# Half-size weight splits in the slots of the first attention, and the first softmax tile's scores ahead of the last lead-in block

## The reference, cut to what matters

```python
z = h @ w_in
c_q, c_kv, k_pe, fq, fk, fv, f_logit = split(z)
q  = (rms_norm(c_q, g_cq) @ w_uq)           # 8 MLA heads, 96 wide
kv = (rms_norm(c_kv, g_ckv) @ w_ukv)        # k_nope, v_mla
o_mla = blocked_causal_attention(q, k, v_mla, scale)
o_fox = blocked_causal_attention(qf, kf, vf, scale, cum_log_f)   # 8 "fox" heads, 64 wide
out = concatenate([o_mla, o_fox]) @ w_out
```

## Time and profile before

| | us |
|---|---|
| median of 3 runs | 1318.15 |
| lowest and highest of them | 1315.78, 1324.64 |
| the profiled execution | 1322.65 |
| its span | 1320.7 |
| PE busy in the span | 1253.3 (95%) |
| DVE busy | 914.6 (69%) |
| ACT busy | 708.5 (54%) |
| mean granted clock of TensorE | 0.976 |

### The profile page before, as it was taken

How to read it: one execution, slowest core, us unless ns; L and a number is a source line. 1 busy time by engine, 2 the same in 40 slices (tenths; PEclk the granted TensorE clock), 3 DMA queues, 4 the chain that set the end, 5 groups by cost and what they waited for, 6 DMA issues and landing times.

```text
span 1320.7 us, 24258 instructions
## 1 busy us (share of the span) xinstructions
PE 1253.3 (95%) x8344; PEld 1136.4 (86%) x8344; DVE 914.6 (69%) x1553; ACT 708.5 (54%) x1257; POOL 259.2 (20%) x277
## 2 busy tenths in 40 slices
PE   7999989999999999999999889999999888999996
PEld 6998889999999888888899668888889866888885
DVE  5778865555557987865666778786558857878563
ACT  4656645654444556654454665664445745666441
POOL 4000012210001034410000003441016511344010
PEclk9999999999999999999999889999999997999998
DMA  7414235655556556555555215555554432665540
GB/s 220 139 41 148 65 96 160 191 177 176 189 159 193 190 161 190 191 191 189 192 185 180 85 33 183 185 188 182 188 181 138 160 96 64 191 187 187 183 143 32
DMA packets 202389, 205.69 MB, mean 156 GB/s; under 512 B 6080, under 2 KB 199734, under 8 KB 202314
## 3 DMA queue, kind: packets, MB, share of 16 engines
q1 hardware_dynamic: 200053, 203.12, 48.1%
q10 hardware_dynamic: 2260, 1.58, 0.4%
HBM read 203.61 MB, written 1.06 MB: 155 GB/s over the span
## 4 chain that ended last, share of the span: by engine, by line
PE 77%; DVE 13%; ACT 5%; issue 3%; POOL 1%; DMA 0%; DVEq 0%; SPq 0%; POOLq 0%; ACTq 0%
PE PS L1521 28%; PE PS L1522 14%; PE PS L1515 10%; PE PS L1516 9%; PE PS L1517 9%; DVE wlo L869 4%; DVE x L846 2%; ACT whi L465 1%; DVE tmp L882 1%; DVE h L892 1%; PE PS L1671 1%; PE PS L1736 1%; PE PS L1714 1%; POOL mt L1491 1%; POOL mqk L1494 1%
## 5 line engine op out<-in xcount | busy, mean ns | idle before, releaser
L869 DVE TENSOR_TENSOR wlo<-raw,whi 128x1024 fp32r<-128x1024 f32 (+1 forms) x388 | 470.5, 1214 | 217.1 <-ACT whi L465 215.3
L465 ACT ACTIVATE whi<-raw 128x1024 fp32r<-128x1024 f32 (+1 forms) x388 | 404.6, 1046 | 333.3 <-PE PS L1522 215.9
L1521 PE MATMUL PS<-x,whi 128*128 128x512 f32 x832 | 293.7, 397 | 4.8 <-DVE x L846 4.5
L1515 PE MATMUL PS<-x,whi 128*128 128x256 f32 (+2 forms) x928 | 269.8, 291 | 10.8 <-DVE x L846 5.8
L1516 PE MATMUL PS<-x,whi 128*128 128x256 f32 (+2 forms) x928 | 267.5, 288 | 0.0
L1521 PE MATMUL PS<-hid,whi 128*128 128x512 f32 x768 | 267.0, 394 | 0.0
L1517 PE MATMUL PS<-x,wlo 128*128 128x256 f32 (+2 forms) x928 | 265.2, 286 | 0.0
L1522 PE MATMUL PS<-x,wlo 128*128 128x256 f32 x832 | 235.1, 283 | 0.0
L1522 PE MATMUL PS<-hid,wlo 128*128 128x256 f32 x768 | 212.7, 277 | 0.0
L1422 POOL TENSOR_TENSOR acc<-acc,sq 128x256 f32<-128x256 f32 (+2 forms) x72 | 63.9, 888 | 717.8 <-ACT sq L493 716.7
L1521 PEld LDWEIGHTS PS<-x,whi 128*128 128x128 f32 x832 | 157.0, 189 | 42.4 <-DVE x L846 6.4
(11 more groups left out here) (286 smaller groups left out, 1616.7 us busy)
## 6 DMA issues: line engine op xcount, KB each, us to landing
raw<-in_mlp_w SPq DMA_DIRECT2D x64, 1024.0 KB, 5.3
raw<-in_w_mlp_up SPq DMA_DIRECT2D x32, 1024.0 KB, 5.5
raw<-in_w_mlp_down SPq DMA_DIRECT2D x32, 1024.0 KB, 4.9
raw<-in_w_in_conv SPq DMA_DIRECT2D x12, 1024.0 KB, 5.1
raw<-in_attn_w_in SPq DMA_DIRECT2D x12, 1024.0 KB, 5.2
raw<-in_mlstm_w_in SPq DMA_DIRECT2D x12, 1024.0 KB, 5.2
raw<-in_w_in_attn SPq DMA_DIRECT2D x9, 1024.0 KB, 5.7
raw<-in_w_out_attn SPq DMA_DIRECT2D x4, 1024.0 KB, 5.4
```

Of the source, the lines that this page charges most:

```text
L465: A(part_view(whi, b), raw_view(b), ACT.Copy).then_inc(w_hi, 1)
L869: V.tensor_tensor(part_view(wlo, b), raw_view(b), f32(part_view(whi, b)), ALU.subtract).then_inc(w_lo, 1)
L1515: mm(dst, whi_b, xs_hi, start=first, stop=False)
L1521: mm(dst.rearrange("p (a t) -> p a t", a=2), std_cols(whi[b % RING], k), xs_both, start=first, stop=False)
```

## The change

It does two things.

First, `a_scores(0)` on PE (with its wait for `fg_sent`), `a_max(0)` on DVE and `a_exp(0)` on ACT (both with their wait for the memsets of POOL) are done within the lead-in loop, at the top of its last turn, ahead of block 12 on PE, ahead of `a_read(12)` on DVE and ahead of the split of block 16 on ACT. The definition of `a_max` moves up with it.

Second, within the slots a split is made in two halves. The high half 0 stands in the slot where the whole split stood, the high half 1 in the slot after. The low half 0 stands in the slot of the high half 1, and the low half 1 one slot later; both wait for `w_hi` of the whole block. Splits outside the slots stay whole.

```diff
+        def half_view(view, half):
+            n = view.shape[1] // 2
+            return view[:, half * n:half * n + n]
...
+            def split_hi_half(b, half):
+
+                if half == 0:
+                    g = blocks[b][1]
+                    act.wait_ge(raw_ready[g % RAW], 16 * (g // RAW + 1))
+                    act.wait_ge(w_used, b - RING + 1)
+                ins = A(half_view(part_view(whi, b), half), half_view(raw_view(b), half), ACT.Copy)
+                if half:
+                    ins.then_inc(w_hi, 1)
...
+                if j == A_LEAD - 1:
+                    act.wait_ge(Z["pool_set"], 10)
+                    a_exp(0)
                 split_hi(B["a_in"] + j + RING)
...
-                if n + 1 < N_A:
+                if 0 < n + 1 < N_A:
                     a_exp(n + 1)
...
-                if n - 1 in USED:
-                    split_hi(USED[n - 1] + RING)
+                for half in range(2):
+                    if n - 1 - half in USED:
+                        split_hi_half(USED[n - 1 - half] + RING, half)
...
+            def split_lo_half(b, half):
+
+                dve.wait_ge(w_hi, b + 1)
+                ins = V.tensor_tensor(half_view(part_view(wlo, b), half), half_view(raw_view(b), half),
+                                      f32(half_view(part_view(whi, b), half)), ALU.subtract)
+                if half:
+                    ins.then_inc(w_lo, 1)
...
+                if j == A_LEAD - 1:
+                    dve.wait_ge(Z["pool_set"], 10)
+                    a_max(0)
                 a_read(j)
...
-                if n - 1 in USED:
-                    split_lo(USED[n - 1] + RING)
+                for half in range(2):
+                    if n - 2 - half in USED:
+                        split_lo_half(USED[n - 2 - half] + RING, half)
...
+                if j == A_LEAD - 1:
+                    pe.wait_ge(Z["fg_sent"], 32)
+                    a_scores(0)
                 a_block(j, range(KB))
...
-            pe.wait_ge(Z["fg_sent"], 32)
-            a_scores(0)
             for n in range(N_A + 2):
```

More of the change, by code:

```diff
@@ L623, in _ @@
                     act.dma_start(ak[FOX:FOX + 1, :, :], fgate[:, 2, :]).then_inc(Z["fg_sent"], 16)
-            act.wait_ge(Z["pool_set"], 10)
             for n in range(-1, N_A + 3):
@@ L1042, in a_read, with a_max @@
                     mul(a_z(z_in(j))[:, 0:T], PS[:, bk, 0:T], rstd[:, :]).then_inc(psum_read, 1)
+            def a_max(n):
+                hd, i, t0, rows, w = a_tile(n)
+                dve.wait_ge(Z["a_s"], n + 1)
+                if n >= 2:
+                    dve.wait_ge(Z["a_exp"], n - 1)
+                V.tensor_tensor_reduce(out=a_sm[0:rows, n % 2, 0:w], in0=PS[0:rows, 2 + n % 2, 0:w],
+                                       in1=amask[0:rows, (NT - 1) * TQ - t0:(NT - 1) * TQ - t0 + w], scale=-1.0, scalar=-3 * NEG,
+                                       op0=ALU.add, op1=ALU.min, accum_out=a_st[0:rows, 1, n:n + 1]).then_inc(Z["a_max"], 1)
             for j in range(A_LEAD):
+                if j == A_LEAD - 1:
+                    dve.wait_ge(Z["pool_set"], 10)
+                    a_max(0)
                 a_read(j)
@@ L1064, in _ @@
                     V.tensor_scalar(gkv[0:NOPE, :], rope[0:NOPE, :], va("g_k_mla", 0, 0, NOPE), None, ALU.mult).then_inc(Z["gq_set"], 1)
[L1067 to L1075, removed]
             def a_turn(n):
```

## The result

The changed kernel takes 1311.84 us (median of 7 runs, 1308.48 to 1314.43), the kernel before 1318.42 in its 7. The ratio is 0.9941, with a 95% interval of 0.9918 to 0.9965, so it is faster, by 0.35 to 0.82%. The forecast was 1315.0 in a range of 1309 to 1321.5, a gain of 3.1 us; the medians differ by 6.6. More runs give steadier numbers: all 19 runs of the changed kernel have a mean of 1312.7 us, and 74 later runs of the kernel before 1319.0, with standard errors of 0.7 and 0.4. The gain is 6.3 us, twice the forecast.

What follows compares the result with a forecast made beforehand. PE was taken as the bound in the first attention, its idle time the most to gain. A 0.6 + B 2.8 - C 0.3 = 3.1 us off the median 1318.15 gave 1315.0 us, range 1309 to 1321.5.

Steps and rivals of the forecast that it cites:

- Term A: First tile moved into the lead-in: 0.6 us gained, bounds 0 and 3.3, with PE's wait moving to tile 1.
- Term B: Half splits shorten PE's waits for the exponential after 72 us: 2.8 us gained, at most 3.7.
- C: Work added on DVE and ACT by halving the splits, mostly hidden in idle time: 0.3 us lost.
- share of 0.77: Gain of 1.06 of the 1.36 us wait at the last tile, applied to five waits totalling 3.7 us.
- the 0.84 at tile 13: PE's wait for the exponential at 101.42 us, forecast to stay because DVE's other work stands ahead of the maximum.
- One sign of being wrong: New waits of PE for ACT between 110 and 150 us would show the forecast wrong.
- the bound of 2.3 us: Upper bound on DVE time added by halving 18 low splits, taking the widest for all.
- the clock: Low clock stretches left as they are in the sum; each one that goes is worth 1.7 us.
- The rival that gains 1.7 or 3.4: Shorter waits let low clock stretches at 68 and 181 us go: 1313.3 to 1311.6 us, chance 0.20.
- The slower rival: First low halves wait for queued high halves, next maximum behind them on DVE: 1321.3 us, chance 0.15.
- Only term A: Maxima come late because of DVE's total work, so the halves give nothing: 1317.5 us, chance 0.20.
- The loads: Later low splits free raw buffers later, but no load is waited for: costed at nothing, at most 5 us.

Runs made afterwards that it cites:

- e3: The changed kernel with the splits kept whole and the low split one slot after the high one; median 1312.13 us, ratio 0.9954.
- e8: The changed kernel once more, with no edit, for a second profile and more runs; median 1313.0 us in 12 runs, ratio 0.9961.
- e7: The changed kernel with a semaphore of its own for the first high half, so the first low half waits only for that; median 1313.65 us, ratio 0.9961.
- e2: The changed kernel with the first tile's scores, maximum and exponential put back behind the lead-in, half splits kept; median 1313.73 us, ratio 0.9961.
- e1: The changed kernel with whole splits back in their old slots, only the first tile moved; median 1317.45 us, ratio 0.9981.

## Why the prediction was right, point by point

**The bound.** PE's idle time was the thing to count. 9.1 us of waits became 5.4, and over the eleven kernels of the table the time follows that sum. The number was right by the width of its range: 3.1 us were forecast and 6.3 measured.

**Term A**, 0.6: the mechanism and the place were right. PE's wait fell from 3.28 to 2.57, by 0.7. The new wait was put at 2.7 us before the transpose of tile 1 and is 2.57; that transpose was put at 68.9 and stands at 68.65, with the lead-in of this execution some 0.04 to 0.2 us earlier. The maximum of tile 1 was to be 0.33 later; counted from the last head sum it is 67.66 - 62.77 = 4.89 against 67.55 - 62.81 = 4.74, so 0.15 later. The split of block 16 starts at 63.37, not 63.59, because DVE came to the maximum 0.22 earlier in this execution (62.64, forecast 62.86); the steps of 0.36 and 0.37 behind it are as forecast. By itself the part measured 1.3 +- 0.8.

**Term B less C**, 2.8 - 0.3 = 2.5: the waits for the exponential after 72 us fell from 4.5 to 1.6, which is 2.9, and the halves alone measured 3.2 +- 0.6, or 3.4 at full clock. At the last tile 1.06 was forecast and 4.41 - 3.36 = 1.05 gained. The new wait before the last output is there too, though without a bracket: that output starts 1.56 us after the transposes, where it was 1.34. But the share of 0.77 gave the right sum by luck. It left 23% of each of the five waits. In fact all five are gone (tiles 17, 35, 39, 43 and 47), waits of 0.46 and 0.55 stand before two tiles that had none (36 and 41), and the 0.84 at tile 13, which was to stay, is 0.63. One sign of being wrong did appear, a new wait of PE for ACT between 110 and 150 us, though a small one:

```profile
138.78 0.70 PE L1700 MATMUL PS<-asq,ones 97*128 97x272 f32 x2 [0.17 <-ACT ars L601]
```

The loss C doesn't show: PE's busy time in the dense stretch rose to 39.50 of 40 us, while DVE is busy 35.91 instead of 34.44. The added work itself was set too low: the bound of 2.3 us took the widest split for all, but halving costs DVE 0.15 us whatever the width, 2.7 in all (21.4 against 18.7 in e3). Whether a part of it reached PE was not measured apart.

But the reason under term B was too narrow. It said what a half gives against a whole. e3 shows that the same is had with whole splits if the low one leaves its slot; what stood in the way was the low split with its wait for the high split, in that slot, ahead of the next maximum; its length alone was not it.

**The sum** was too small by 3.2 us, in two places. The order gave 4.2 (estimate at full clock) to 4.3 (span times clock) where A + B - C had 3.1; PE's bracketed waits account for 3.7 of it. And **the clock** was kept as it was, at nothing. The rest of the 6.3, once 0.2 outside the span is taken off (1.73 us against 1.95), is 1.8 us: span less span times clock fell from 27.5 to 25.7, with an error of 1.1. If a us of that is worth only 0.6 us of time, as among the runs of the kernel before, the clock gave 1.0 and the order more, 5.3. So the clock's part is likely, not shown beyond its error. The rival that gains 1.7 or 3.4 was perhaps right in part, with a chance of 0.20; the row that spoke against it (a low stretch after a wait of 1.36 us) shows that such a stretch can come, and e8 against the first profile shows that it needn't. It should have entered as a chance in the sum and not as all or nothing. By the rule of the Trainium skill (Perfetto Trace Analysis, Matmul Optimizations: power follows utilization, keep matmuls back to back) the clock had to gain from shorter waits. The traces agree in direction, a low stretch from 68 to 72 us behind five of seven waits of over 2.5 us and behind none of six of at most 1.53. The changed kernel, though, only shortened its wait from 3.28 to 2.57, and at 2.57 three of five profiles are low.

**The slower rival** fell. DVE's waits for high splits stayed at 5.2 us, as forecast near 5, and what they cost, 1.56 us by e7 at full clock, is less than the halves gain. **"Only term A"** fell with e2. The loads were never late: no high split waits for one.

## What to carry to other kernels

When an operation is moved out of a wait, follow the queues of all three engines to the next wait: a gap of 3.28 us became one of 2.57 a slot later, and only taking two head norms (2 us) out of DVE's queue cut it to 0.48. Before cutting a piece of work in two, try it in a later slot: here that gave the same time with 18 fewer instructions on each of two engines. With two profiles of different length in hand, look at the clock before explaining the difference: of the 14 us between these two, span less span times clock accounts for 9.5 (31.7 and 22.2 us). The sum of PE's waits, and a stretch that has the full clock in both, compare better than the whole.

## What the runs showed of the hardware

The granted clock after a wait is made likely by the wait, but not fixed by it. After the same wait of 2.57 or 2.58 us the stretch from 68 to 72 us had 1.00 in one execution of the changed kernel and in e7, 0.78 in the other execution of the changed kernel, 0.58 in e3 and 0.50 in e1; after waits of 0.47 to 1.53 us it had 1.00 in all six profiles. Shorter waits didn't rule out a low stretch elsewhere: after 0.63 and 0.69 us near 100 us the changed kernel had 1.00 in one execution and 0.62 in the other.

PE's waits themselves repeat to 0.01 us between the two profiles of the changed kernel, while its attention took 111.79 us in one and 114.87 in the other. Most of the spread of the runs goes with the clock: the kernel before ranges over 11.6 us in its later runs, 1313.82 to 1325.43, and the correlation of a run's time with its span less span times clock is 0.94. One us of the latter goes with 0.6 us of time; why less than one was not measured.
